# Sparse attention scores from split operands stacked to 128 rows, built by GpSimd per head, in a two-layer mixer step

## What is computed

```python
vals, idx = lax.top_k(idx_score, topk)
kg = jax.vmap(lambda kb_, ib_: kb_[ib_])(k, idx)
logits = jnp.einsum('bqgrd,bqkgd->bqgrk', q, kg).astype(jnp.float32) * DSA_SCALE
logits = jnp.where(valid[:, :, None, None, :], logits + bias, -jnp.inf)
p = jax.nn.softmax(logits, axis=-1).astype(vg.dtype)
```

## Time and profile before

| | |
|---|---|
| time, median of 3 runs | 1264.71 us (1260.44 to 1266.16) |
| span of the profiled execution | 1255.0 us (its own total is not listed) |
| TensorE matmul busy | 1131.9 us, 90% |
| TensorE weight load busy | 982.9 us, 78% |
| VectorE busy | 783.6 us, 62% |
| ScalarE busy | 486.3 us, 39% |
| GpSimd busy | 388.6 us, 31% |
| granted clock of TensorE, mean | 0.952 |

### The profile page before, as it was taken

One profiled execution on the slowest core, in us unless ns is written; L12 is line 12 of the kernel. 1 busy time (PEld: TensorE's weight loads), 2 busy tenths in 40 slices (PEclk: granted clock), 3 DMA queues, 4 the chain that ended last, 5 costly groups with the idle time before them and its releaser, 6 DMA issues. The chain is left out here.

```text
span 1255.0 us, 20340 instructions
## 1 busy us (share of the span) xinstructions
PE 1131.9 (90%) x7644; PEld 982.9 (78%) x7660; DVE 783.6 (62%) x1626; ACT 486.3 (39%) x1088; POOL 388.6 (31%) x220
## 2 busy tenths in 40 slices
PE   3189999999999999989979999999999999988996
PEld 2067698677888888879967779777888888878995
DVE  7964899572447875254646489965235786535555
ACT  4344545532443333332324544633244343332322
POOL 5633265021122322233334235502112222223332
PEclk9589799999999999989999989999999999999998
DMA  9624022121114444113424303221111454311353
GB/s 376 220 87 132 14 88 68 55 68 34 34 34 152 153 155 155 60 40 115 166 99 128 91 19 100 64 63 47 34 42 53 156 173 152 118 51 51 110 179 150
DMA packets 39066, 128.17 MB, mean 102 GB/s; under 512 B 5736, under 2 KB 6344, under 8 KB 38128
## 3 DMA queue, kind: packets, MB, share of 16 engines
q1 hardware_dynamic: 36496, 122.04, 29.5%
q10 hardware_dynamic: 2464, 4.74, 1.0%
HBM read 117.41 MB, written 11.58 MB: 103 GB/s over the span
## 5 line engine op out<-in xcount | busy, mean ns | idle before, releaser
L688 PE MATMUL pj<-h_hi,w_hi 128*128 128x272 f32 x1776 | 526.4, 296 | 13.3 <-DVE h_lo L1488 6.1
L690 PE MATMUL pj<-h_lo,w_hi 128*128 128x272 f32 x1776 | 517.3, 291 | 0.0
L689 PE MATMUL pj<-h_hi,w_lo 128*128 128x272 f32 x1776 | 514.4, 290 | 0.0
L1591 POOL TENSOR_TENSOR w_lo<-ring,w_hi 128x1024 fp32r<-128x1024 f32 x112 | 275.6, 2461 | 584.7 <-ACT w_hi L1033 584.6
L688 PEld LDWEIGHTS pj<-h_hi,w_hi 128*128 128x128 f32 x1776 | 339.0, 191 | 17.4 <-POOL w_lo L1591 6.6
L689 PEld LDWEIGHTS pj<-h_hi,w_lo 128*128 128x128 f32 x1776 | 339.0, 191 | 0.2
L690 PEld LDWEIGHTS pj<-h_lo,w_hi 128*128 128x128 f32 x1776 | 337.7, 190 | 0.0
L1033 ACT ACTIVATE w_hi<-ring 128x1024 fp32r<-128x1024 f32 x112 | 119.1, 1063 | 144.1 <-PE pj L690 130.8
L1480 DVE CUSTOM_DVE_ANT_0 squares<-ring,silu_c 128x1024 f32<-128x1024 f32 x96 | 128.3, 1336 | 7.0 <-DMA ring<-in_wts 5.3
L1179 ACT ACTIVATE probs<-logit,negmax 128x128 f32<-128x128 f32 (+2 forms) x68 | 39.1, 575 | 198.9 <-DVE negmax L1422 184.9
L1413 DVE TENSOR_REDUCE negmax<-ps 128x1 f32<-128x128 f32 (+1 forms) x64 | 31.4, 490 | 107.1 <-PE ps L883 106.9
(11 more groups left out here) (239 smaller groups left out, 1541.6 us busy)
## 6 DMA issues: line engine op xcount, KB each, us to landing
ring<-in_wts SPq DMA_DIRECT2D x167, 512.0 KB, 3.6
wide<-x_between SPq DMA_DIRECT2D x4, 1088.0 KB, 5.6
x_between<-wide ACTq DMA_DIRECT2D x16, 272.0 KB, 2.5
wide<-in_wts SPq DMA_DIRECT2D x3, 1024.0 KB, 20.8
ring<-in_wts SPq DMA_DIRECT2D x6, 384.0 KB, 2.9
wide<-in_xT SPq DMA_DIRECT2D x1, 2176.0 KB, 13.2
x_between<-in_xT SPq DMA_DIRECT2D x1, 2176.0 KB, 9.8
bias_p<-in_wts SPq DMA_DIRECT2D x2, 1024.0 KB, 7.8
```

The source lines that it names most:

```text
L688: pe.matmul(out, hi, h_hi[:, k, half(b)], start=(k == first), stop=False)
L689: pe.matmul(out, lo, h_hi[:, k, half(b)], start=False, stop=False)
L690: return pe.matmul(out, hi, h_lo[:, k, half(b)], start=False, stop=(k == stop))
L1591: pool.tensor_tensor(w_lo[:, slot, :], w(*splits[n]), w_hi[:, slot, :].bitcast(F32), ALU.subtract).then_inc(s_wlo, 1)
```

## The change

The sparse score becomes two fp32r matmuls of 128 rows. `qst` holds a head's queries, the rounding in the rows of its group and the remainder in the other 64; `kst` holds for each group two tiles, the rounded keys in both halves, and the remainder in both halves. hi and lo of the queries meet first the rounded keys, then the remainder. GpSimd builds both: the keys once per layer, eight chained operations of 64 partitions and 512 columns, and the queries by a copy and a subtraction per head, each waited for, into two buffers by turns. TensorE waits for `s_kst` once and for `s_qst` at the first block of each head. Both share the memory of the four sample tiles. kb moves ahead of qb in the order of the projections, so that the tiles are now: 17 kb, 18 to 21 qb.

```diff
@@ def fillers()
-    f += [("qb", t, b) for t in range(4) for b in range(2)] + [("kb", 0, b) for b in range(2)]
+    f += [("kb", 0, b) for b in range(2)] + [("qb", t, b) for t in range(4) for b in range(2)]
@@ buffers
-        ck_s = sb("ck_s", [P, 2, NT])
-        cv_s = sb("cv_s", [P, 5, KVL])
-        kr_s = sb("kr_s", [P, NT])
+        shared_at = nc.sbuf_base
+        shared = sb("shared", [P, 2 * NT + 5 * KVL + NT + 2 * NH * TS])
...
+        kst = nc.alloc_sbuf_tensor_at("kst", [P, 2, 2, TP], F32R, offset=shared_at)
+        qst = nc.alloc_sbuf_tensor_at("qst", [P, 2, TP], F32R, offset=shared_at + 4 * 4 * TP)
...
-        qa_s = sb("qa_s", [P, 2, NH * TS])
@@ TensorE, scores, kind "dp"
-                            rows = slice(64 * (h // 4), 64 * (h // 4) + 64)
-                            pe.matmul(out[:, 0:n], qb[rows, h % 4, P * (NQ - 1 - i):P * (NQ - i)], kb[rows, 0:n],
-                                      start=True, stop=False)
+                            if h == 0 and i == 0:
+                                pe.wait_ge(s_kst, 1)
+                            if i == 0:
+                                pe.wait_ge(s_qst, h + 1)
+                            for part in range(2):
+                                pe.matmul(out[:, 0:n], qst[:, h % 2, P * (NQ - 1 - i):P * (NQ - i)],
+                                          kst[:, h // 4, part, 0:n], start=(part == 0), stop=False)
@@ GpSimd, after the last gate
-                    rest(5)
+                    rest(2)
...
+                    def link(ins):
+
+                        chain[0] += 1
+                        ins.then_inc(s_pch, 1)
+                        pool.wait_ge(s_pch, chain[0])
+
+                    pool.wait_ge(s_wlo, split[0])
+                    pool.wait_ge(s_qkb, 2)
+                    pool.wait_ge(s_pv, last_ms + 1)
+                    for g in range(2):
+                        own, other = slice(64 * g, 64 * g + 64), slice(64 - 64 * g, 128 - 64 * g)
+                        link(pool.tensor_copy(kst[own, g, 0, :], kb[own, 0:TP]))
+                        link(pool.tensor_copy(kst[other, g, 0, :], kb[own, 0:TP]))
+                        link(pool.tensor_tensor(kst[own, g, 1, :], kb[own, 0:TP], kst[own, g, 0, :].bitcast(F32), ALU.subtract))
+                        link(pool.tensor_tensor(kst[other, g, 1, :], kb[own, 0:TP], kst[own, g, 0, :].bitcast(F32), ALU.subtract))
+                    pool.sem_inc(s_kst, 1)
+                    rest(3)
+                    pool.wait_ge(s_wlo, split[0])
                     pool.wait_ge(s_qkb, 10)
+
+                    def stack_queries(h):
+
+                        own = slice(64 * (h // 4), 64 * (h // 4) + 64)
+                        other = slice(64 - 64 * (h // 4), 128 - 64 * (h // 4))
+                        if h >= 2:
+                            pool.wait_ge(s_sco, steps.index(("dp", h - 2, NQ - 1)) + 1)
+                        pool.wait_ge(s_wlo, split[0])
+                        link(pool.tensor_copy(qst[own, h % 2, :], qb[own, h % 4, 0:TP]))
+                        link(pool.tensor_tensor(qst[other, h % 2, :], qb[own, h % 4, 0:TP], qst[own, h % 2, :].bitcast(F32),
+                                                ALU.subtract))
+                        pool.sem_inc(s_qst, 1)
+
+                    stack_queries(0)
+                    rest()
+                    stack_queries(1)
+                    rest()
                     pool.tensor_copy(kb_s[:, TP:NT], kb[:, TP:NT]).then_inc(s_gch, 1)
                     pool.tensor_copy(qb_s[:, :].rearrange("p (a q) -> p a q", a=4), qb[:, :, TP:NT]).then_inc(s_gch, 1)
-                    rest(16)
+                    rest()
+                    for h in range(2, NH):
+                        stack_queries(h)
+                        rest(2)
+                    rest()
```

More of the change, by code:

```diff
@@ L235, in build @@
         ckv = sb("ckv", [P, 2, NT])
-        ck_s = sb("ck_s", [P, 2, NT])
-        cv_s = sb("cv_s", [P, 5, KVL])
-        kr_s = sb("kr_s", [P, NT])
+        shared_at = nc.sbuf_base
+        shared = sb("shared", [P, 2 * NT + 5 * KVL + NT + 2 * NH * TS])
+        ck_s = shared[:, 0:2 * NT].rearrange("p (c t) -> p c t", c=2)
+        cv_s = shared[:, 2 * NT:2 * NT + 5 * KVL].rearrange("p (k c) -> p k c", k=5)
+        kr_s = shared[:, 2 * NT + 5 * KVL:3 * NT + 5 * KVL]
+        qa_s = shared[:, 3 * NT + 5 * KVL:3 * NT + 5 * KVL + 2 * NH * TS].rearrange("p (c n) -> p c n", c=2)
+        kst = nc.alloc_sbuf_tensor_at("kst", [P, 2, 2, TP], F32R, offset=shared_at)
+        qst = nc.alloc_sbuf_tensor_at("qst", [P, 2, TP], F32R, offset=shared_at + 4 * 4 * TP)
         kr = sb("kr", [P, NT])
@@ L564, in build @@
         s_oat = sem("sample_values_applied")
+        s_kst = sem("stacked_keys_ready")
+        s_pch = sem("pool_stack_chain")
+        s_qst = sem("stacked_queries_ready")
         s_oev = sem("output_bank_read")
@@ L575, in build @@
                   s_kr8, s_wi, s_isc, s_irl, s_iac, s_sel, s_gin, s_gad, s_gat, s_lat, s_lsq, s_lst, s_lrt, s_lno,
-                  s_ctc, s_kv, s_qn, s_qrw, s_qsw, s_qr, s_qap, s_qac, s_sco, s_max, s_exp, s_pro, s_ptt, s_ptc, s_pv, s_oat,
+                  s_ctc, s_kv, s_qn, s_qrw, s_qsw, s_qr, s_qap, s_qac, s_sco, s_max, s_exp, s_pro, s_ptt, s_ptc, s_pv, s_oat, s_kst, s_pch, s_qst,
                   s_oev, s_qkb, s_mth, s_m, s_xup, s_vch, s_ach, s_gch, s_out]
@@ L1637, in _ @@
                         rest()
-                    rest(5)
-                    pool.wait_ge(s_qkb, 10)
+                    rest(2)
+                    chain = [0]
+                    def link(ins):
[11 more added lines that the diff above has]
+                        link(pool.tensor_tensor(kst[other, g, 1, :], kb[own, 0:TP], kst[own, g, 0, :].bitcast(F32), ALU.subtract))
```

## The result

The change took 1267.03 us (median of 9 runs), the kernel before 1259.38 in the runs beside it; the ratio is 1.0053, with an interval of 1.0034 to 1.0072. The forecast was 1256, a gain of 8.4 us; the ratio is worth a loss of 6.7. The profiled execution took 1267.03 for a span of 1264.9: 2.1 us lie around a span (1.8 in runs of the kernel before), not the 9.7 that I had read out of a median over three scattered runs.

What follows compares the result with a forecast made beforehand. TensorE was taken to bound the sparse part, VectorE next. Per layer -16.5 + 5.8 + 2.5 + 3.0 + 1.0 = -4.2, for two -8.4 us: span 1246.6, time 1256 us, own range 1250 to 1262, outer 1246 to 1268.

Steps and rivals of the forecast that it cites:

- Saved by the matmuls: Sparse scores: cheaper fp32r matmuls save 2.07 us per head, 16.5 us per layer.
- The 0.3 us of the 64 rows: Each sparse step: about 0.3 us is no streaming, ascribed to the operand that fills only half the rows.
- The first stall: First sparse step: TensorE waits for a GpSimd split and stacking pair, starting 5.8 us later per layer (5.4 to 6.8).
- the clock: After the first sparse step's wait: TensorE drops to half speed, costing 2.5 us per layer (1.7 to 3.4).
- Later heads: Heads 1 to 3: each waits about 1.0 us for GpSimd's stacking, 3.0 us per layer (0.5 to 5).
- the term for VectorE: Sparse steps in which TensorE comes to wait for VectorE: 1.0 us per layer (0 to 2).
- The base: Starting time: median 1264.71 us, span 1255.0, so 9.7 us taken to lie around the span.
- outer range of 1246 to 1268: Whole kernel: time range in us that reaches into both cases neighbouring the forecast's own 1250 to 1262.
- all given back: Rival: stall 6.8, clock 3.4, heads 5, VectorE 1.5, so +0.2 us per layer, 1265 us; chance 0.22.
- the one with the 0.3 us unchanged: Rival, sparse scores: the 0.3 us stays, only 7.8 saved, +4.5 us per layer, 1274 us; chance 0.04.
- GpSimd's pair as the pace: Rival, first sparse step and later heads: at 4.5 us per stacking pair the time is 1275 us; chance 0.05.
- signs of being wrong: Pair far from 2.1 us, a clock that holds, 0.3 us still there, or VectorE ending most of TensorE's waits.

Runs made afterwards that it cites:

- e4: Kernel before the change, its fp32 score matmul taken over 128 rows with zero-filled keys; 1247.41 us, ratio 0.9882.
- e9: e5 with one correction: the queries of heads 6 and 7 stacked one split later; 1238.99 us, ratio 0.9828 to the kernel before.
- e5: Changed kernel with GpSimd's list reordered so that queries are stacked earlier, same operations; 1254.64 us, ratio 0.9946 to the kernel before.
- e13: Changed kernel with only head 0's stacking pair moved, to after the split of tile 21; 1246.60 us, ratio 0.9906 to the kernel before.
- e2: Changed kernel with each VectorE product with an ada tile over half its columns; 1244.09 us, ratio 0.9871 to the kernel before.
- e14: e9 with each VectorE product with an ada tile over half its columns; 1231.72 us, ratio 0.9757 to the kernel before.

## Why the prediction was wrong

- **Saved by the matmuls**, 16.5 us per layer: right. 2.07 per head, 0.59 at 512 columns, 0.48 at 384 and 0.30 at 128 against forecasts of 0.58, 0.47 and 0.30. The 0.3 us of the 64 rows was confirmed by e4 (0.28).
- **The first stall**, 5.8: right. TensorE waited 7.65 us instead of 1.80, 5.85 more; it came to the wait itself 0.26 later than before, and started at 379.29. The pair took from 377.15 to 379.10, 1.95 us. The clock fell as forecast (0.55 granted over 380 to 384 us). Head 0 took 20.17 and 20.22, against 17.29 in e9, so 2.9 more; but 0.76 of that is the wait for head 1's pair, which ends the distance:

```profile
399.46 0.41 PE L901 MATMUL ps<-kst,qst 128*128 128x128 f32 x2 [0.76 <-POOLq L1682]
```

  That leaves **2.1** for the clock, instead of 2.5. The expectations of e5 and e13 count the whole 2.9 as cold work. In e2, which keeps the stall and relieves VectorE, head 0 takes 19.01 and 19.15, against 17.28 in e14: 1.7 and 1.9 more, 0.2 of it a wait for GpSimd.
- **Later heads**, 3.0 for GpSimd and 1.0 for VectorE: this is the step that failed, and in it the term for VectorE. GpSimd's waits past the first came to 2.9 us in layer 0 (0.76 and 2.12) and 0.76 in layer 1. But against the floor of e14, heads 1 to 3 lost 4.7 + 2.8 + 1.6 = 9.1 us in layer 0 and 5.0 + 4.3 + 2.9 = 12.2 in layer 1. With the 0.76 at head 1's first score that is 9.9 and 12.9, not 4.0 each; without GpSimd's waits, 7.0 and 12.2 for VectorE and the clock behind its waits, not 1.0 each. Over both layers these terms were 14.8 us too small and the one for the clock 0.7 too large, which turns a forecast of -8.4 into +5.7; the measured ratio is worth +6.7.
- **How it failed.** I compared averages, VectorE's idle time of over a microsecond per step against 0.5 less, and called the rest slack. The row I needed was one instruction's deadline: L1464 at 406.75 for a product at 408.38, once per head, behind 2.5 us of products:

```profile
406.75 0.68 DVE L1464 TENSOR_TENSOR gate_b<-po,gate_b 64x512 f32<-64x512 f32 x1
...
408.38 0.39 PE L946 MATMUL po<-pT,vb 128*128 128x128 f32 x2
```

  With steps 0.5 us shorter, a late tile or a split on the port in that step became bare waits of 2.6 to 3.1 us, and behind three of these four the granted clock fell.
- **The base.** The forecast stood on 9.7 us around the span, and about 2 was right. From the true base of 1259 the same sum would have said 1251; it moved the number, not the sign. 1267 lies at the upper edge of the outer range of 1246 to 1268, but that range was counted from 1265: its edge meant a loss of 3 us, and the loss is 6.7.
- **The rivals.** The nearest in time, all given back at 1265 us, came near by luck: its stall of 6.8, clock of 3.4 and 5 for the heads are all above what was measured (5.85, 2.1, and 2.9 and 0.76), and its 1.5 for VectorE is far below 7.0 and 12.2. Of the two that ended slower, the one with the 0.3 us unchanged fell with the 0.59 us above. The other had GpSimd's pair as the pace. It took up to 3.9 us at head 3 (437.31 to 441.19), with VectorE in the way, but the bare waits for it behind the first stall stayed small. None had VectorE's queue for its cause; it was named as next in line, and among the signs of being wrong.

No run kept the stall and the clock apart, so the clock's 2.1 us is what is left over and not a measurement by itself. In the later heads, too, the wait for VectorE and the clock behind it weren't separated. A version with VectorE's products shortened without leaving work out wasn't tried.

## What to carry to other kernels

When the bounding engine gets 10% faster in a step (19.29 to 17.22 us a head here), the next engine must be judged by its deadlines inside one step, not by its mean: find the instruction of it that the fast engine waits for soonest, and what is queued ahead. Ahead of building an operand on a free engine, look where in that engine's list the building stands: here moving one pair by two splits was worth 1.5%. And before splitting an operand to fill the rows, try filling them with zeros: that gave 1.2% (1.5% with kb first) with no new work per head, against 1.7% for the whole scheme in its best order, and the runs can't tell these last two apart.

## What the runs showed of the hardware

- An fp32 score over 64 rows cost 0.28 us more than the same columns over 128 rows, standing between 128-row matmuls (1.26 and 0.98 us to the mask); its weight load and the next one started late (at 387.59 and 388.64) and were not longer.
- Two fp32r matmuls at 128 columns took 0.09 us each (0.30 less 0.125, for two), the middle that the forecast took between 0.065 and 0.107.
- A GpSimd copy that rounds 512 columns to fp32r takes 0.60 us undisturbed; beside VectorE's two-input products it took up to 1.69, and the subtraction 2.15 instead of 1.27.
- TensorE's clock fell after most of its short waits, not after all. In heads 1 to 3 of the change the waits of 2.85 us (ending at 416.55), 2.12 (441.39), 3.12 (1014.13) and 2.63 (1035.74) were followed by a stretch at half clock (1.2 GHz): the granted clock was 0.72 over 416 to 420 us, 0.66 over 441 to 446, 0.64 over 1014 to 1018 and 0.66 over 1035 to 1040. The one of 2.61 at 1057.28 was not (1.00 over 1050 to 1072). Waits of 1.81 us at the first sparse step went both ways in e13 (0.72 over 960 to 966, 1.00 over 374 to 380). A projection matmul stands 0.125 us from the next at full clock (2.4 GHz) and 0.22 at half (381.60 to 381.82, behind the first stall).
